# Two decoder layers with mixture-of-experts: attention's buffers share places, gate and up run in four column tiles, the gather goes through four banks

## The chip, the core and the metric

The kernel runs on one core of one Trainium2 chip. The metric is the device time of one execution in microseconds, the median of the runs shown. In the profile, PE is TensorE (PEld its weight loads), DVE is VectorE, ACT is ScalarE, POOL is GpSimd, and SP is SyncE, whose queue issues nearly all DMAs of this kernel. Times inside the trace count from the start of the span.

## The reference

Two post-norm layers work on 256 tokens of width 1024, all in float32. Layer 0 mixes tokens by sliding-window attention with sinks, layer 1 by differential attention; in both, four more heads attend to 256 memory tokens. After `x = LN(alpha*x + mix)` comes the expert block, and then `x = LN(alpha*x + moe)`. Cut to what matters here:

```python
aff = sigmoid(x @ w_router)                  # 64 experts, 8 groups
eidx = top 8 experts of the 4 best groups    # for each token
gates = aff[eidx] / sum(aff[eidx]) * 2.5
for every expert e and the tokens that chose it:
    h = silu(xb @ w_gate[e]) * (xb @ w_up[e])        # 1024 -> 256
    routed += gate * (h @ w_down[e])                 # 256 -> 1024
shared = (silu(x @ ws_gate) * (x @ ws_up)) @ ws_down
moe = routed + shared
```

Each expert has three matrices of 1 MB (1024 x 256 float32). With 64 experts and two layers that is 403 MB of the 449 MB that the kernel moves.

## The kernel before, in words

**The ring.** `store` holds the router's matrix `wr` and then 12 places of one matrix each (`ring`). Experts are worked on in pairs; a pair is one unit, and a layer has 32 of them. Even units take their six matrices from places 6 to 11, odd units from places 0 to 5 (`pair_place`, L134): two gates, two ups, two downs (`matrix_at`). So the ring holds two units. Besides it there are a few places of their own: `apart` (unit 1's second down), `up_apart` in `work` (unit 0's first up), and the four buffers `home`, `lnrow`, `xT`, `x` with `memT`, which take over one whole pair, number 16, once attention and routing have no more use for them (`keep`, L553). In steady state a place is loaded again as soon as its matrix has been used (`reload_gate`, `reload_up`, `reload_down`, L453 to L495).

**Before the experts.** During attention the same ring places hold the projection matrices (`in0` to `in3`, `memkv`, `out0`, `out1`) and the shared expert's gate and up (`shared`). Which place each has stands in `first_place` (L130), and `before_it` says after which other item it may be loaded. SP walks this list in order (L604 to L650), and each of its waits holds back everything behind it in the list. What the attention leaves occupied is loaded late: unit 1's two gates wait for the second logit group and for the end of the shared expert's up (L642, L644, semaphore `gate_apart`); `xT` and `x` are free last (L556).

**One unit on PE** (`unit`, L1410): `gate` (L1282 to L1305), `up` (L1307 to L1332), `scatter` of the unit two before (adds rows back into the token sums, L1372), `turn_back` for the next unit (L1264 to L1269), `turn_h` (L1337, transposes of the hidden rows), on every fourth unit `gather` of the next eight experts' tokens (L1236 to L1258), and `down` of the unit before (L1341 to L1366). For `gate` and `up` the stationary operand is the 64 token slots of an expert, so two experts sit side by side in two tiles of 64 columns; `down` works with tiles of 32 columns, four side by side. A float32 matmul shows up as two records in the trace, so a `gate` has 32 matmul records and 32 weight loads.

**The gather** writes eight chunks of x into PSUM banks 0, 1, 2, 0, 1, 2, 0, 1; ACT copies the even chunks out, DVE the odd ones. A chunk waits until the last one in its bank has been copied. `down` behind a gather waits for the copies of the last chunks (`xg_act` and `xg_dve`), since it writes to banks 0 and 1.

**The first reloads.** PE reports the first half of a gate (`half_gated`), and SP then loads unit 2's first gate half into the same place (`reload_gate_halves`, L521 and L523). This is the earliest load that depends on the experts' own progress.

The trace shortens some names: L848 is `product`, used for the gather and others; L1498 and L1742 are the copies of ACT and DVE.

Of the kernel before, what the change touches and what calls it, by code (L numbers as in the profile page):

```python
# [78 lines left out]
def build_trunk(nc, x_in, xT_in, memT_in, w_in_a, sinks, w_in_b, lambda_qk, subln_g, w_mem_kv, w_out, ln_g, ln_b,  # L79
# [43 lines left out]
    for l in range(DEPTH):  # L123
# [10 lines left out]
    before_it = [{"out1": "in0", "shared": "in1"}, {"out0": "memkv", "out1": "in2", "shared": "in0"}]  # L134
    pre = [[(l, name) for name in first_place[l]] for l in range(DEPTH)]
# [4 lines left out]
    with ExitStack() as ctx:  # L140
# [11 lines left out]
        store = sb("store", [P, KT * NE + 2 * REGION * MATRIX])  # L152
        wr = store[:, 0:KT * NE].rearrange("p (k n) -> p k n", k=KT)
        ring = store[:, KT * NE:]
        router_gate = store[:, 0:KT * (NE + HID)].rearrange("p (c k n) -> p c k n", k=KT, n=NE)
# [6 lines left out]
        work_at = nc.sbuf_base  # L162
        work = sb("work", [P, 8960])
# [5 lines left out]
        qT = work[:, 0:1536].rearrange("p (t n) -> p t n", n=SEQ)  # L169
        kT = work[:, 1536:3072].rearrange("p (t n) -> p t n", n=SEQ)  # L170
        v = work[:, 3072:4608].rearrange("p (t n) -> p t n", n=768)
        qmT = work[:, 4608:5120].rearrange("p (t n) -> p t n", n=SEQ)
        kmT = work[:, 5120:5632].rearrange("p (t n) -> p t n", n=MEM)
        vm = work[:, 5632:6144].rearrange("p (t n) -> p t n", n=MEM_HEADS * HD)
        mixT = work[:, 6144:8192].rearrange("p (t n) -> p t n", n=SEQ)
        heads = over("heads", [P, TT, 768], xhalf_at + 8192)
# [5 lines left out]
        yhalf = over("yhalf", [P, 2, D], work_at + 4 * 5120, F32R)  # L182
        yend = [work[:, 5120 + c:5120 + c + 256] for c in (512, 768)]
        hot8 = over("hot8", [P, TT, OCTET * TILE_SLOTS], work_at + 4 * 7168, F32R)
# [3 lines left out]
        sgs = work[:, 3584:4096].rearrange("p (t n) -> p t n", t=TT)  # L188
        hsrow = work[:, 7680:8192].rearrange("p (t n) -> p t n", t=TT)
# [6 lines left out]
        soft = [over(f"soft{i}", [P, 256], xhalf_at + 1024 * i) for i in range(3)] + [work[:, 8450:8706]]  # L196
        softT = [over(f"softT{i}", [P, 2, P], xhalf_at + at) for i, at in enumerate((4096, 5120, 14336, 15360))]
# [9 lines left out]
        negdist = over("negdist", [P, 2 * P], xhalf_at + 3072)  # L207
        apart = sb("apart", [P, FT, D])
        up_apart = work[:, 5120:7168].rearrange("p (k n) -> p k n", k=KT)
# [6 lines left out]
        lamrow = over("lamrow", [P, 4, HD], xhalf_at + 6144)  # L216
        sublnrow = over("sublnrow", [P, 2 * HD], xhalf_at + 7168)
        lamv = sb("lamv", [P, 8])
        lamp = over("lamp", [P, 2, HD], xhalf_at + 7680)
# [7 lines left out]
        passed = work[:, 5120:6144]  # L227
        route = sb("route", [P, 4, TT, NE])
# [29 lines left out]
        gather_bank = (0, 1, 2, 0, 1, 2, 0, 1)  # L258
# [14 lines left out]
        def item_loads(it):  # L273
# [6 lines left out]
            if name == "shared":  # L280
                return [(matrices(at), ws_gate[l]), (by_k(matrices(at + 1)), by_row_run(ws_up[l]))]
            if name[:3] == "out":
                return [(matrices(at, 2), w_out[l, int(name[3])])]
# [45 lines left out]
        def last_group(it):  # L329

            l, name = it
            return G[l, {"memkv": "vm", "in0": "q2" if l == 0 else "q5", "in1": "qm" if l == 0 else "k5", "in2": "vd", "in3": "qm",
                         "out0": "y2", "out1": "y3"}[name]]
# [11 lines left out]
        def used(sp, it):  # L345

            if it[1] == "shared":
                sp.wait_ge(sem(f"shared_gu_{it[0]}"), TT)
            else:
                filled(sp, last_group(it))  # L350
# [25 lines left out]
        def bank_at(g):  # L376
            return banks[bank_no[g]]
# [40 lines left out]
        def _(sp):  # L418
# [120 lines left out]
            def next_down(l):  # L539

                sp.dma_start(apart[:], w_down[l, 1, :, 1, :].rearrange("p (f n) -> p f n", f=FT)).then_inc(sem("down_apart"), 16)
                sp.sem_inc(sem(f"down_landed{RING - 1}_{l}"), 16)
                expert(l, 1, RING - 1, 2)
# [34 lines left out]

            extra = None
            for l in range(DEPTH):  # L580
                for it in pre[l]:
                    if it[1] in before_it[l]:
                        used(sp, (l, before_it[l][it[1]]))
                    elif l > 0:

                        of_pair = 0 if place_of[it] >= REGION else 1
                        sp.wait_ge(sem(f"down_done_{l - 1}"), extra * NE + (NE - RING + 2 * of_pair + 2))
                    if it == (1, "memkv"):
                        load_part(it, 0)
                        load_memory_halves()  # L590
                        load_norm(1, extra)
                        load_part(it, 1)
                    else:
                        load(it)
                    if it == (1, "in3"):
                        sp.wait_ge(sem("x_back"), TT)
# [1536 lines left out]
```

## Time and profile before

| | before |
|---|---|
| runs, us | 1186.79, 1184.7, 1186.67 |
| median, us | 1186.67 |
| span of the profiled execution, us | 1183.3 |
| median less span (what lies around the span), us | 3.4 |
| PE busy | 1149.2 us, 97% |
| DMA | 449.12 MB, mean 380 GB/s |
| granted clock of TensorE, mean | 0.996 |

The span is one profiled execution; durations below come from it. A PE that is busy 97% of the time is not a PE at its peak, since the ends of pipelined matmuls are modelled. The slices of the page show the DMA rate over the span: near 428 GB/s through both expert phases, and two stretches with far less, which are the two attentions.

### The profile page before, as it was taken

Reading aid. Unit: us, or ns where it says so; the run is one execution under the profiler, and the core shown is the slowest. Engines: PE = TensorE matmul, PEld = TensorE weight load, DVE = VectorE, ACT = ScalarE, POOL = GpSimd, SP = SyncE. Lnnn points to the kernel's source line nnn. Section 1 sums busy time; section 2 is a strip of 40 time slices with the busy share of each in tenths; the row PEclk is TensorE's granted clock in tenths of the full one; section 3 lists DMA queues with packets and bytes.
Section 4 is the critical chain, followed back from the end, with each engine's and each line's share of the span. In section 5 each row is a group of like instructions: output and inputs, shape, how many; then the busy total and the mean of one; then the engine's idle time right before and its main releaser. Section 6 shows DMA issues by size and latency. Waiting matters only on the chain.

```text
span 1183.3 us, 22174 instructions
## 1 busy us (share of the span) xinstructions
PE 1149.2 (97%) x8846; PEld 688.0 (58%) x8846; DVE 347.2 (29%) x912; ACT 300.0 (25%) x713; POOL 56.4 (5%) x100
## 2 busy tenths in 40 slices
PE   9999999999999999999999999999999899999995
PEld 6865755555555555554787647555555555555552
DVE  0445522222122212121523557221222222121224
ACT  1454222212122212121214533122221212221222
POOL 1431100000001000000011001000000010000000
PEclk9999999999999999999999999999999999999998
DMA  9945999999999999999990558999999999999995
GB/s 375 418 161 185 349 418 426 428 428 428 429 428 421 429 426 427 426 426 418 406 364 2 230 233 343 408 426 426 429 429 428 428 423 427 426 426 428 428 423 204
DMA packets 42732, 449.12 MB, mean 380 GB/s; under 512 B 4512, under 2 KB 4896, under 8 KB 14240
## 3 DMA queue, kind: packets, MB, share of 16 engines
q1 hardware_dynamic: 41648, 443.30, 89.8%
q10 hardware_dynamic: 1008, 4.73, 1.0%
q8 instruction: 57, 0.93, 0.3%
q14 instruction: 19, 0.16, 0.0%
HBM read 446.96 MB, written 1.05 MB: 379 GB/s over the span
## 4 chain that ended last, share of the span: by engine, by line
PE 85%; DMA 9%; DVE 3%; ACT 1%; issue 1%; DVEq 0%; SPq 0%; ACTq 0%
PE bank L1301 18%; PE bank L1328 17%; PE bank L1364 17%; PE bank L848 7%; PE bank L867 6%; PE bank L1372 5%; PE bank L906 4%; DMA store<-in_w_gate 4%; DMA store<-in_w_down 3%; DMA store<-in_w_in_b 2%; PE bank L1337 2%; PE bank L1196 1%; PE bank L1066 1%; PE bank L1077 1%; ACT work L1498 1%
## 5 line engine op out<-in xcount | busy, mean ns | idle before, releaser
L1301 PE MATMUL bank<-store,work 128*64 128x256 f32 x1984 | 227.8, 382 | 5.3 <-DMA store<-in_w_gate 5.3
L1328 PE MATMUL bank<-store,work 128*64 128x256 f32 x1952 | 225.3, 379 | 6.2 <-issue 6.2
L1364 PE MATMUL bank<-store,work 128*32 128x512 f32 x1888 | 218.4, 595 | 3.1 <-ACT work L1498 2.9
L1301 PEld LDWEIGHTS bank<-store,work 128*64 128x64 f32 x1984 | 137.0, 137 | 116.1 <-issue 41.1
L1328 PEld LDWEIGHTS bank<-store,work 128*64 128x64 f32 x1952 | 145.0, 137 | 75.7 <-issue 11.6
L2030 DVE SCALAR_TENSOR_TENSOR yhalf<-bank,gcol,yhalf 128x512 fp32r<-128x512 f32 x124 | 92.9, 751 | 219.1 <-ACT yhalf L1664 219.1
L2022 DVE TENSOR_TENSOR work<-work,bank 128x256 f32<-128x256 f32 x64 | 27.0, 422 | 346.9 <-PE bank L1328 346.9
L1664 ACT ACTIVATE yhalf<-bank,gcol 128x512 fp32r<-128x512 f32 x124 | 85.1, 688 | 172.1 <-PE bank L1364 172.1
L1364 PEld LDWEIGHTS bank<-store,work 128*32 128x32 f32 x1888 | 56.1, 109 | 122.4 <-issue 110.7
L1498 ACT ACTIVATE work<-bank 128x512 f32<-128x512 f32 (+4 forms) x177 | 78.0, 441 | 105.8 <-PE bank L848 47.3
L1498 ACT ACTIVATE back<-bank 128x128 fp32r<-128x128 bf16 x64 | 17.8, 278 | 282.0 <-PE bank L1269 282.0
L867 PE MATMUL bank<-xT,store 128*128 128x256 f32 x352 | 77.9, 380 | 0.7 <-DMA store<-in_w_in_b 0.7
L1372 PE MATMUL bank<-yhalf,back 64*128 64x512 f32 x504 | 75.7, 418 | 0.0
L1742 DVE COPY work<-bank 128x512 f32<-128x512 f32 (+3 forms) x77 | 51.5, 672 | 70.8 <-PE bank L848 41.2
L867 PEld LDWEIGHTS bank<-xT,store 128*128 128x128 f32 x352 | 66.2, 190 | 10.4 <-DMA store<-in_w_in_b 1.1
L1654 ACT ACTIVATE work<-bank 128x256 f32<-128x256 f32 x64 | 24.6, 385 | 184.3 <-PE bank L1301 184.3
L848 PE MATMUL bank<-hot,xhalf 128*128 128x256 f32 x512 | 69.4, 290 | 1.0 <-DVE xhalf L1895 0.9
L848 PEld LDWEIGHTS bank<-hot,xhalf 128*128 128x128 f32 x512 | 64.0, 189 | 4.6 <-issue 2.1
L1372 PEld LDWEIGHTS bank<-yhalf,back 64*128 64x128 f32 x504 | 42.4, 184 | 30.1 <-issue 23.8
L906 PE MATMUL bank<-store,work 128*128 128x512 f32 x128 | 57.8, 594 | 0.0
L906 PEld LDWEIGHTS bank<-store,work 128*128 128x128 f32 x128 | 23.2, 190 | 23.4 <-issue 23.1
L819 POOL TENSOR_TENSOR x<-xhalf 128x1024 f32<-128x1024 f32 x4 | 9.6, 2426 | 475.3 <-PE bank L1364 475.3
(185 smaller groups left out, 822.7 us busy)
## 6 DMA issues: line engine op xcount, KB each, us to landing
store<-in_w_down SPq DMA_DIRECT2D x56, 2048.0 KB, 17.7
store<-in_w_gate SPq DMA_DIRECT2D x56, 2048.0 KB, 17.7
store<-in_w_up SPq DMA_DIRECT2D x52, 2048.0 KB, 19.2
store<-in_w_up SPq DMA_DIRECT2D x18, 1024.0 KB, 10.5
store<-in_w_gate SPq DMA_DIRECT2D x12, 1024.0 KB, 8.5
store<-in_w_in_b SPq DMA_DIRECT2D x3, 3072.0 KB, 22.4
store<-in_w_out SPq DMA_DIRECT2D x4, 2048.0 KB, 14.2
store<-in_w_down SPq DMA_DIRECT2D x6, 1024.0 KB, 11.7
```

The lines of the kernel that those rows point to most:

```text
L848: last = pe.matmul(dst, a, b, start=(n == 0), stop=(n == len(pairs) - 1))
L867: mm = pe.matmul(bank_at(g)[:, c * 256:(c + 1) * 256], w[:, k, c0 + c * P:c0 + (c + 1) * P], moving[:, k, :], start=(k == 0), stop=(k == K ...
L906: last = pe.matmul(bank_at(g)[:], mixT[:, c, t * P:(t + 1) * P], item_view((l, f"out{half}"), 512)[:, c, :], start=start, stop=(done == KT))
L1301: last = pe.matmul(gate_bank[slots_of(e), 0:HID], xg[:, k, slots_of(2 * j + e)], w[e][:, k, :], start=(k == 0), stop=(k == KT - 1))
L1328: last = pe.matmul(up_bank[slots_of(e), 0:HID], xg[:, k, slots_of(2 * j + e)], w[e][:, k, :], start=(k == 0), stop=(k == KT - 1))
L1364: last = pe.matmul(yb[half][rows_of(t, e), :], hT[b][:, f, slots_of(e, t)], w[e][:, f, half * 512:half * 512 + 512], start=(f == 0), stop= ...
L1372: pe.matmul(sums[2 * t + half][:], back[b][rows_of(t), :], yhalf[rows_of(t), n, half * 512:half * 512 + 512], start=False, stop=False)
L1498: return act.activation(dst, src, ACT.Copy)
L1664: act.activation(yhalf[:, 0, half * 512:half * 512 + 512], yb[half][:], ACT.Copy, scale=gcol[:, j:j + 1])\
L1742: return dve.tensor_copy(dst, src)
L2022: dve.tensor_tensor(hidrow, sg, up_bank[:, 0:HID], ALU.mult).then_inc(s_("h_ready"), 1)
L2030: dve.scalar_tensor_tensor(out=yhalf[:, 1, part], in0=yb[half][:], scalar=gcol[:, j:j + 1], in1=yhalf[:, 0, part].bitcast(F32), op0=ALU.mu ...
```

## The change

It does four things.

1. The router's matrix moves out of `store` to the front of `work`; the ring keeps its 12 places. The soft-max buffers, `heads`, `negdist` and the like move from `xhalf` into `work`, and the row constants of layer 1 onto `route`. `xhalf` so becomes free during attention and holds the first half of the output projection (`out_first`, in place of `out0`).
2. The shared expert's gate and up go to `work[0:4096]` (where keys, values and memory keys and values lie until attention is done) in place of ring places.
3. SP's list is written out by hand for each layer. Experts' matrices whose places are now free are loaded earlier in it, among them unit 1's two gates as one load. The loads `gate_apart` and `gate_landed` behind the logits are gone.
4. On PE, `gate` and `up` issue one matmul for each 32 slots, four column tiles in place of two. The gather uses banks 0, 3, 1, 2, 0, 3, 1, 2, and the waits in and behind it are set accordingly.

The core of the diff:

```diff
-        {"in1": 0, "in0": 3, "memkv": 6, "out0": 8, "out1": 3, "shared": 0},
-        {"memkv": 6, "in1": 9, "in0": 0, "in3": 8, "in2": 3, "out0": 6, "out1": 3, "shared": 0},
+        {"in1": 0, "in0": 3, "memkv": 6, "out1": 3},
+        {"memkv": 6, "in1": 9, "in0": 0, "in3": 8, "in2": 3, "out1": 3},
...
+        out_first = over("out_first", [P, KT, 512], xhalf_at)
+        shared_w = [work[:, 0:MATRIX], work[:, MATRIX:2 * MATRIX]]
...
-        gather_bank = (0, 1, 2, 0, 1, 2, 0, 1)
+        gather_bank = (0, 3, 1, 2, 0, 3, 1, 2)
...
+            def load_shared_down(l):
+                sp.wait_ge(sem("softened"), sum(len(jobs[i]) for i in range(l + 1)))
+                sp.dma_start(shared_wd, by_row_pair(ws_down[l])).then_inc(sem("shared_wd_landed"), 16)
+
+            def load_shared(l):
+                sp.dma_start(shared_w[0], ws_gate[l]).then_inc(sem("shared_gate_landed"), 16)
+                sp.dma_start(by_k(shared_w[1]), by_row_run(ws_up[l])).then_inc(sem("shared_up_landed"), 16)
+
+            def first_layer():
...
+                load_out_first(0)
+                load_rows(0)
+                row_pair(0)
+                load_x()
+                pair(0, 0, 0, 2)
+                next_up(0)
+                expert(0, 0, 1, 1)
+                load_apart(0)
+                used(sp, (0, "in0"))
+                load((0, "out1"))
+                next_down(0)
+                used(sp, (0, "in1"))
+                pair(0, 0, 1, 0)
+                expert(0, 0, 2, 1)
+                for e in range(2):
+                    keep(0, 0, e)
+                used(sp, (0, "memkv"))
+                pair(0, 0, 0, 0)
+                keep(0, 2, 1)
+                load_shared_down(0)
+                sp.wait_ge(sem("valued"), len(products[0]))
+                load_shared(0)
+                load_up_apart(0)
+
+            def second_layer(extra):
...
+                load((1, "in2"))
+                load_out_first(1)
+                load_apart(1)
+                for e in range(2):
+                    keep(1, 0, e)
+                used(sp, (1, "memkv"))
+                pair(1, 0, 0, 0)
+                keep(1, 2, 1)
+                sp.wait_ge(sem("normed"), 2 * TT)
+                row_pair(2)
+                used(sp, (1, "in3"))
+                next_up(1)
+                used(sp, (1, "in2"))
+                load((1, "out1"))
+                next_down(1)
+                used(sp, (1, "in1"))
+                expert(1, 0, 1, 1)
+                pair(1, 0, 0, 2)
+                used(sp, (1, "in0"))
+                pair(1, 0, 1, 0)
+                expert(1, 0, 2, 1)
+                load_shared_down(1)
+                filled(sp, G[1, "heads"] + 2)
+                load_shared(1)
+                load_up_apart(1)
...
                 used(sp, (l, "out1"))
                 expert(l, 0, 3, 1)
                 expert(l, 0, 2, 2)
                 sp.wait_ge(sem("normed"), 2 * TT * l + TT)
-                load_up_apart(l)
                 keep(l, 1, 0)
-                filled(sp, G[l, "vm"])
-                keep(l, 2, 1)
-                filled(sp, G[l, "logit1"])
-                sp.dma_start(matrices(matrix_at(1, 0, 0)), w_gate[l, 1, :, 0, :]).then_inc(sem("gate_apart"), 16)
-                used(sp, (l, "shared"))
-                sp.dma_start(matrices(matrix_at(1, 1, 0)), w_gate[l, 1, :, 1, :]).then_inc(sem(f"gate_landed{UNROLL}_{l}"), 16)
+                sp.wait_ge(sem(f"shared_gu_{l}"), TT)
                 keep(l, 1, 1)
...
-                landed(pe, it)
+                pe.wait_ge(sem("shared_gate_landed"), (l + 1) * 16)
...
+                pe.wait_ge(sem("shared_up_landed"), (l + 1) * 16)
                 up_shared(0)
...
                         if k == 2 and backs is not None:
-                            pe.wait_ge(s_("hT_ready"), backs)
-                        if k == 1 and backs is not None:
                             pe.wait_ge(s_("back_ready"), backs + 1)
                             pe.wait_ge(s_("gcol_ready"), backs + 1)
+                        if k == 3 and backs is not None:
+                            pe.wait_ge(s_("hT_ready"), backs)
...
                         for e in range(2):
-                            last = pe.matmul(gate_bank[slots_of(e), 0:HID], xg[:, k, slots_of(2 * j + e)], w[e][:, k, :],
-                                             start=(k == 0), stop=(k == KT - 1))
+                            for t in range(TT):
+                                last = pe.matmul(gate_bank[slots_of(e, t), 0:HID], xg[:, k, slots_of(2 * j + e, t)], w[e][:, k, :],
+                                                 start=(k == 0), stop=(k == KT - 1))
...
-                        if half == 0:
-                            pe.wait_ge(s_("xg_act"), 4 * gathers + 1)
-                        else:
-                            pe.wait_ge(s_("xg_dve"), 4 * gathers + 1)
+                        pe.wait_ge(s_("xg_act"), 4 * gathers + half)
+                        if half == 1:
```

`up` is changed as `gate` is, with `up_bank`. ACT's copy of x into `xhalf` (`x_high`) has a new wait, for the third output group `y2`, since `out_first` lies there.

## Rows read from the trace of the kernel before

**Rows 1.** The page: DMA rate in 40 slices of the span.

```profile
GB/s 375 418 161 185 349 418 426 428 428 428 429 428 421 429 426 427 426 426 418 406 364 2 230 233 343 408 426 426 429 429 428 428 423 427 426 426 428 428 423 204
```

**Rows 2.** Busy time in stretches: layer 0's units 4 to 7, 8 to 11, 12 to 15.

```profile
core 0: us, PE busy (x) PEld busy (x) DVE busy (x) ACT busy (x) POOL busy (x), PEclk, DMA share, GB/s
182.60:235.90 53.30, 53.09 (x468) 29.81 (x464) 12.72 (x30) 12.10 (x24) 0.00 (x0) 1.00 1.01 426
235.90:289.20 53.30, 53.11 (x468) 30.18 (x464) 12.63 (x30) 12.09 (x24) 0.00 (x0) 1.00 1.01 428
289.20:347.90 58.70, 53.85 (x468) 30.86 (x464) 12.65 (x30) 12.08 (x24) 0.00 (x0) 1.00 1.01 429
```

**Rows 3.** Groups of PE instructions, 289.2 to 347.9 us: busy, mean ns, idle before.

```profile
L1364 PE MATMUL bank<-store,work 128*32 128x512 f32 x132 | 15.2, 595 | 0.2 <-ACT work L1498 0.2
L1301 PE MATMUL bank<-store,work 128*64 128x256 f32 x128 | 14.7, 382 | 1.8 <-DMA store<-in_w_gate 1.8
L1328 PE MATMUL bank<-store,work 128*64 128x256 f32 x128 | 14.6, 381 | 2.9 <-issue 2.9
```

**Rows 4.** The chain that ended last, in order of time: start, length, what.

```profile
1137.99 18.08 DMA store<-in_w_down
```

**Rows 5.** SP's issues about the start of layer 0's experts: start, length, line.

```profile
129.52 0.33 SPq L644 DMA_DIRECT2D store<-in_w_gate  x1
129.89 0.43 SPq L556 DMA_DIRECT2D xT<-in_w_up  x1
132.15 0.33 SPq L556 DMA_DIRECT2D x<-in_w_down  x1
136.28 0.68 SPq L521 DMA_DIRECT2D store<-in_w_gate  x1
```

**Rows 6.** Busy time in two stretches there, columns as in rows 2.

```profile
130.00:138.00 8.00, 7.64 (x64) 5.94 (x64) 4.72 (x11) 2.40 (x4) 3.51 (x6) 1.00 0.94 357
138.00:142.00 4.00, 3.95 (x36) 2.33 (x35) 0.60 (x4) 0.57 (x3) 0.00 (x0) 1.00 0.97 321
```

**Rows 7.** DMA issues from 103.0 to 103.6 us, 136 to 137, 734 to 735: time to landing.

```profile
store<-in_w_up SPq DMA_DIRECT2D x1, 1024.0 KB, 5.0
...
store<-in_w_gate SPq DMA_DIRECT2D x1, 1024.0 KB, 8.4
...
store<-in_w_gate SPq DMA_DIRECT2D x1, 1024.0 KB, 9.5
```

**Rows 8.** Instruction blocks among the DMAs of units 4 to 7 (182.6 to 235.9 us).

```profile
q8 instruction: 4, 0.07, 0.5%
```

**Rows 9.** DMA kinds of units 8 to 11 (235.9 to 289.2 us).

```profile
q1 hardware_dynamic: 1566, 22.81, 100.6%
q14 instruction: 1, 0.01, 0.0%
```

**Rows 10.** PE groups by shape: the last down's halves, four tiles of 32 columns.

```profile
L1397 PE MATMUL bank<-store,work 128*32 128x256 f32 x64 | 3.9, 379 | 0.0
```

**Rows 11.** PE in order of time: a gate, its up, the down behind, the next gate.

```profile
182.83 3.67 PE L1301 MATMUL bank<-store,work 128*64 128x256 f32 x32
186.33 3.62 PE L1328 MATMUL bank<-store,work 128*64 128x256 f32 x32
...
191.49 3.64 PE L1364 MATMUL bank<-store,work 128*32 128x512 f32 x32
195.06 1.30 PE L1301 MATMUL bank<-store,work 128*64 128x256 f32 x10
```

**Rows 12.** PE's end of attention in order of time, layer 0, then layer 1.

```profile
95.12 1.09 PE L1100 MATMUL bank<-softT,work 128*64 128x128 f32 x16
...
110.88 4.47 PE L1179 MATMUL bank<-store,xT 128*128 128x320 f32 x16
...
690.73 0.60 PE L1139 MATMUL bank<-ident,heads 128*128 128x128 f32 x4
...
709.23 3.12 PE L1179 MATMUL bank<-store,xT 128*128 128x320 f32 x11
```

More of the change, by code:

```diff
@@ L279, in item_loads @@
                 return parts if l == 1 else [(matrices(at, 2), w_mem_kv[l].rearrange("j p n -> p j n"))]
[L280 to L283, printed above, removed]
+            if name == "out1":
+                return [(matrices(at, 2), w_out[l, 1])]
             if it == (0, "in1"):
@@ L618, in _ @@
                 if l == 0:
-                    used(sp, (0, "memkv"))
-                    pair(0, 0, 0, 0)
-                else:
-                    used(sp, (1, "in1"))
-                    expert(1, 0, 1, 1)
-                    pair(1, 0, 0, 2)
-                sp.wait_ge(sem("softened"), sum(len(jobs[i]) for i in range(l + 1)))
-                sp.dma_start(shared_wd, by_row_pair(ws_down[l])).then_inc(sem("shared_wd_landed"), 16)
-                used(sp, (l, "out0"))
-                if l == 0:
-                    next_up(0)
-                    expert(0, 0, 1, 1)
-                else:
-                    pair(1, 0, 0, 0)
+                    first_layer()
+                else:
+                    second_layer(extra)
@@ L899, in out_part @@
                     if n not in y_begun:
-                        landed(pe, (l, f"out{half}"))
+                        if half == 0:
+                            pe.wait_ge(sem("out_first_landed"), (l + 1) * 16)
+                        else:
+                            landed(pe, (l, "out1"))
                         bank_free(pe, g)
+                    wo = item_view((l, "out1"), 512) if half else out_first
                     for c in cs:
@@ L905, in out_part @@
                         done = y_done[n] = y_done[n] + 1
-                        last = pe.matmul(bank_at(g)[:], mixT[:, c, t * P:(t + 1) * P],
-                                         item_view((l, f"out{half}"), 512)[:, c, :], start=start, stop=(done == KT))
+                        last = pe.matmul(bank_at(g)[:], mixT[:, c, t * P:(t + 1) * P], wo[:, c, :], start=start, stop=(done == KT))
                         if done == KT:
@@ L1295, in gate @@
                     for k in range(KT):
-                        if j == 0 and k == 0 and first:
-                            chunk_out(O, 3)
+                        if j == 0 and k == 0:
+                            chunk_out(O, 3 if first else 5)
                         if j == 0:
@@ L1327, in up @@
                         for e in range(2):
-                            last = pe.matmul(up_bank[slots_of(e), 0:HID], xg[:, k, slots_of(2 * j + e)], w[e][:, k, :],
-                                             start=(k == 0), stop=(k == KT - 1))
+                            for t in range(TT):
+                                last = pe.matmul(up_bank[slots_of(e, t), 0:HID], xg[:, k, slots_of(2 * j + e, t)], w[e][:, k, :],
+                                                 start=(k == 0), stop=(k == KT - 1))
                         if place == 1 and k == KT // 2 - 1:
@@ L1590, in head_out @@
                     else:
[L1591 removed]
+                        act.activation(heads[:, h, n, :], src, ACT.Copy, scale=rden[:, j - 1:j])
                         act.wait_ge(sem("headed"), m)
```

141 lines of the change are left out of this document (59 added, 82 removed).

## The prediction

> **What bounds the kernel now.** The page's slices come first [rows 1]: both expert phases run at 426 to 429 GB/s, and in each attention the rate falls far below, to 161 and to 2. So there is idle DMA time in attention, which is what earlier loads could use. The question is whether what bounds the experts is PE or the DMA. Busy time in stretches answers it [rows 2]: units 4 to 7 and 8 to 11 take 53.3 us each with PE busy almost throughout, while the DMA share is 1.01 in all three stretches, and units 12 to 15 take 58.7 us for the same 468 matmuls. PE is thus a little faster than the loads; it lives on the two units that the ring held at the start, and when that lead is used up it waits, 1.8 us ahead of gates and 2.9 us ahead of ups [rows 3]. Since the DMA engines are never idle from the first reload on, the end of such a phase is set by the bytes and by when the saturated stretch began, and PE's pace only decides where the waiting is done. The chain of waits agrees [rows 4]: the end of layer 1 goes through a down's load, 18.08 us from issue to landing. Layer 0 has the same order of loads at its end and layer 1's projections queued behind them, so I take both phases to end behind the DMA.
>
> **The change part by part.**
>
> **Earlier loads.** Per layer the bytes are the same, so a load that is moved counts only if it takes bytes out of the saturated stretch. That stretch starts with the first reload, which can't move: SP issues it at 136.28 us, when PE has done half of the first gate [rows 5]. What still lay ahead of it? Three loads of 1024 KB, issued at 129.52, 129.89 and 132.15, 3.15 MB together [rows 5]. From 130 to 138 us the engines moved 357 GB/s x 8 us = 2.86 MB [rows 6], so 0.29 MB, 0.7 us at 428 GB/s, were left at 138, and the reload began at about 138.7. A lone 1 MB load lands 5.0 us after its issue [rows 7], of which 2.45 us is the transfer; of the 2.55 us of the rest I give 1.0 to the time before the first bytes, so the reload could begin at 137.3 at best. The change takes the first of the three loads (L644, unit 1's second gate) out; the other two, 2.1 MB, need 4.9 us from 130.9 and are done by 136. The gain is 138.7 - 137.3 = **1.4 us per layer**, not the 2.45 us of the load itself, and much less than the several MB that are moved in the list: the rest of them only fill time in which the engines have nothing to do anyway. Bounds: nothing, if the second reload, which also waits for PE, leaves a hole; and at most 3.4 us in layer 0 and 4.5 in layer 1, by which the first reload lands later than the lone load (8.4 and 9.5 against 5.0 [rows 7]). I take the value by bytes, because the reload's own pieces move at only 321 GB/s [rows 6], which explains the rest of its lateness without a queue.
>
> **More instructions.** Four tiles double the matmuls and weight loads of gate and up: 32 + 32 records more for each, 128 more per unit, 512 per four units. Four units now issue 468 + 464 records [rows 2] and fetch four blocks of instructions, 0.5% of the engines' 53.3 us, 0.27 us, or 0.067 us a block [rows 8]. 512 on top of 932 make 2.2 blocks more per four units. Units 8 to 11 are the second pass of a loop and fetch none on q8 [rows 9], so six of the eight groups of four fetch: 13 blocks, 0.9 us per layer of saturated DMA. Bounds: nothing, and 1.7 us if the second and third passes (units 8 to 15) also fetch their 6.2 blocks each. The Trainium skill, "Runtime: NRT & Kernel Launch", section "Instruction fetch mechanics", says in a note that there are only two lines of 16 KB and that a taken branch out of them forces a fetch before execution goes on. By that units 8 to 11 would have fetched before too; the trace differs, and the row decides; by the page the sum would be 1.7 us later.
>
> **Four column tiles on PE.** The streaming is the same: as many columns, twice the tiles, each half as wide. The nearest row is the last down's two halves, the very form that gate and up get: 64 records in 3.9 us over two layers [rows 10], so 1.95 us for eight groups of four, less 0.16 us for the modelled end of the last, 0.22 us a group. A gate now has 16 steps in 3.50 us, 0.22 each [rows 11]. What is saved is the change of tile width: gate to up, same width, 3.50 us; down to gate 3.57 us, and that gate's first loads stand free. I take 0.1 us per unit, 3 us per layer, bounds 0 and 0.2.
>
> **Gather and its waits.** Down waits 0.2 us for ACT's copy behind a gather [rows 3], and the fourth bank removes about as much inside it: 0.4 us in seven gathers, some 3 us per layer. `down`'s first half then waits for chunk 4 alone. Neither this nor the tiles reaches the end: they make PE faster in a phase that ends behind the DMA, so they come out as longer waits for gates and ups. I cost them at nothing; what covers them is those waits, 5.4 us in units 12 to 15 already. Only behind the layer's last load is PE alone: there one change from down to up goes, 0.1 us once, in layer 1.
>
> **New waits.** SP now waits for the last values (layer 0) or the last turned heads (layer 1) before the shared gate is issued, and behind that wait stand `up_apart`, unit 1's last up and down, and the keeps. The last values end at 96.2 us, so the load lands at about 101.2; PE needs it at 110.88 for the logits, 9.7 us later [rows 12]. In layer 1: 691.3 + 5.0 = 696.3 against 709.23, 12.9 us. Moved loads ahead of it would have to hold the queue for that long, four MB; so nothing. ACT's wait for `y2` costs nothing either: ACT waits for the first norm there, which follows y0 and y1, and PE runs y2 right behind them. The moved buffers change no instruction's shape.
>
> **Sum.** Two layers: 2 x (-1.4 + 0.9) - 0.1 = -1.1 us. The profiled span of 1183.3 becomes 1182.2; with the 3.4 us that lie between span and median, 1186.67 becomes **1185.6 us**. That is under 0.2% (2.4 us), about the least that a measurement of this kernel can tell from no change.
>
> **The rivals.**
>
> A, the queue was the whole lateness: the first reload lands 3.4 and 4.5 us earlier, and all loads behind it too. For it: the engines were hardly idle from 131 us on, and PE's faster units could free places sooner. Against it: the 321 GB/s. -7.9 + 1.8 - 0.1 = -6.2: 1180.5 us.
>
> B, the longer loop no longer stays where the fetched one stayed: units 8 to 15 fetch too, 2 x 12.4 x 0.067 = 1.7 us more: 1187.3 us, and more if PE also stands at the loop's end. Against it: nothing in rows 8 and 9 tells how much room there is.
>
> C, slower: PE can't be fed with eight instructions per group over a whole gate and up, 256 in a row, where the row of the same form has 64 in a row per layer. The densest long run that waits on nothing visible is 16 matmuls with their loads in 1.09 us [rows 12], 34 ns an instruction; at that pace a group takes 0.27 instead of 0.22 us. 128 gates and ups of 16 groups are 2048 groups: 113 us, less the cover of at least 5.4 + 3 + 3 us per layer, 23 us: +90, 1277 us. It decides from 23 / 2048 = 11 ns per group on. Against it: rows 10 show no such pace. The Trainium skill, "TensorE: Matmul & The Clock Gate", section "Step-by-step: what each phase is for", tells of about 62 ns for a matmul where the sequencer's software decodes it; four would take 0.248 us a group, and the estimate by that page is 1186.67 + 2048 x 0.03 - 23, about 1225 us. The 0.22 us of rows 10 speak against that case here, though only in a short run.
>
> **How the numbers follow.** Forecast (between the bounds of its two terms, 1183 to 1187) 0.57, A 0.22, B 0.13, C 0.05, the rest 0.03 for a shared load that comes late. Faster by over 0.2%: A, and the edge of the forecast where the fetch costs nothing (-2.8 - 0.1), 0.30 together. Slower: C, the rest and the end of B where PE stands at the loop, 0.12. The range takes in A and B and their spread and leaves out C: 1180.3 to 1188.8 us.
>
> **What would show it.** Right: the first reload in each layer lands 1 to 2 us sooner after its issue; the DMA share stays 1.0 from there on; gate and up keep 3.5 us; the octets with PE ahead fall from 53.3 to about 52.5 us while PE's waits for gates and ups grow by as much; q8 counts about a third more blocks. Wrong: gates of more than 3.7 us (C), q8 blocks in the loop's later passes (B), a first reload at 5 us from issue to landing (A), or a phase whose DMA share falls below 1, which would mean that PE bounds it after all.

## The result: 4 us slower, and the profile after

The changed kernel took 1190.17 us (median of 5 runs, 1189.13 to 1190.6) against 1186.03 us for the kernel before (5 runs, 1184.38 to 1186.79): a ratio of 1.0040, 95% interval 1.0029 to 1.0051 (the two medians alone give 1.0035). The forecast was 1185.6 us, within 1180.3 to 1188.8. The profiled execution has a span of 1188.7 us and a time of 1190.48 us; the spans of the two profiles are 5.4 us apart. In the runs on record the time is some 1.8 us over the span. So the 3.4 us that the table ahead of the prediction puts around the span are 1.8 us of that and 1.6 us by which the profiled execution of the kernel before was under its median; against the median of five it is 0.9 us under, and the profile after is 0.3 us over its own. That is why the profiles are further apart than the medians (4.1 us).

Most of what the prediction named as a sign came out as it said, and yet the time went the other way. First the stretches that answer to [rows 2]: units 4 to 7, 8 to 11 and 12 to 15 of layer 0. Four units, eight experts, are called an octet below.

```profile
core 0: us, PE busy (x) PEld busy (x) DVE busy (x) ACT busy (x) POOL busy (x), PEclk, DMA share, GB/s
181.70:233.90 52.20, 52.20 (x724) 28.36 (x720) 12.68 (x30) 12.08 (x24) 0.00 (x0) 1.00 1.01 426
233.90:289.10 55.20, 52.76 (x724) 28.86 (x720) 12.62 (x30) 12.08 (x24) 0.00 (x0) 1.00 1.01 428
289.10:347.90 58.80, 53.31 (x724) 29.07 (x720) 12.75 (x30) 12.08 (x24) 0.00 (x0) 1.00 1.01 429
```

PE is faster: 52.2 us for an octet in which it does not wait, where it took 53.3. It reaches the loads sooner and then waits for them, 2.4 us already in units 8 to 11, and unit 16 starts at 347.9 us, 0.2 us sooner than before. The groups of PE instructions of 289.1 to 347.9 us (busy, mean ns, idle before) answer to [rows 3].

```profile
L1389 PE MATMUL bank<-ring,router_work 128*32 128x512 f32 x132 | 15.2, 595 | 0.0
L1355 PE MATMUL bank<-ring,router_work 128*32 128x256 f32 x256 | 14.6, 380 | 3.7 <-issue 3.7
L1327 PE MATMUL bank<-ring,router_work 128*32 128x256 f32 x256 | 14.6, 380 | 1.8 <-DMA ring<-in_w_gate 1.8
```

Twice the products in the same 14.6 us: no slower issue, so rival C is out. The wait inside the down is gone (0.2 in [rows 3], 0.0 here), the wait ahead of the ups has grown. In PE's order of time two gates whose loads are late show the pace of the loads, one gate to the next with the idle time in brackets:

```profile
315.84 3.66 PE L1327 MATMUL bank<-ring,router_work 128*32 128x256 f32 x64 [0.90 <-DMA ring<-in_w_gate]
...
330.51 3.66 PE L1327 MATMUL bank<-ring,router_work 128*32 128x256 f32 x64 [0.89 <-DMA ring<-in_w_gate]
```

14.67 us for a unit of three loads of 2 MB, 4.89 us a load: this pace of full DMA engines is used below. The first reload of each layer, issue to landing, answers to the last two of [rows 7]: 6.5 and 6.3 us instead of 8.4 and 9.5.

```profile
ring<-in_w_gate SPq DMA_DIRECT2D x1, 1024.0 KB, 6.5
...
ring<-in_w_gate SPq DMA_DIRECT2D x1, 1024.0 KB, 6.3
```

The kinds of DMA: the whole span of the kernel before and of the changed one, then the changed one's units 4 to 7 (as [rows 8]) and 8 to 11 (as [rows 9]):

```profile
q8 instruction: 57, 0.93, 0.3%
...
q8 instruction: 81, 1.33, 0.5%
...
q8 instruction: 6, 0.10, 0.8%
...
q1 hardware_dynamic: 1626, 23.64, 100.6%
q14 instruction: 1, 0.01, 0.0%
```

81 blocks of PE's instructions, where the kernel before has 57. Units 8 to 11 still fetch none, so rival B is out as well: the loop is read once, on its first pass (units 4 to 7: 6 blocks, 4 before). The other new blocks lie in code that runs once. The chain that ended last shows what has become of the time, before and after:

```profile
PE 85%; DMA 9%; DVE 3%; ACT 1%; issue 1%; DVEq 0%; SPq 0%; ACTq 0%
```

```profile
PE 78%; DMA 16%; DVE 3%; issue 2%; ACT 1%; POOL 0%; DVEq 0%; SPq 0%; POOLq 0%; ACTq 0%
```

**Where the 5.4 us lie.** Take the landings of the same loads in both profiles (issue plus time to landing) and subtract. A load that lands at 161.2 us before lands 1.1 us sooner after; the last load of 2 MB before the phase's end (548.8 before) 1.6 later. So layer 0's experts lose 2.7 us on the way. Layer 1's experts start 2.3 us late, 0.7 of it lost at the change of layers (no run here says by what); the first reloads win 0.5 back (+1.8 at 764.2), and the phase loses 3.3 again (+5.1 at 1146.3). The losses are along the two phases, with DMA engines that count as full in both kernels; the rest of the 5.4, 0.3 us, lies behind the phase. Between 232 and 349 us, and between 840 and 952 in layer 1, the landings keep their distance to those of before within 0.05 us: there the four tiles run from the loop and no block comes. So it is not the four streams as such; it is where blocks come.

For all kernels below that leave the loads' order alone, count how far the loads of a phase fall behind their pace: from a load near 161 us to one near 550 (and 766 to 1150) lie 76.5 to 78.5 loads of 2 MB; their time less 4.893 us each is the lag. Worked out from the landings and the list of blocks:

```
                                    blocks in the stretch   lag, us
                                    layer 0  layer 1        layer 0  layer 1
before                                19       18             3.4      2.9
e1   two tiles again                  19       19             3.7      3.6
e6   kept pair at unit 20             23       23             3.9      4.4
e11  before, own code                 27       27             5.5      4.7
e7   kept pair at 20, code as after   29       29             5.7      5.1
e3   columns cut                      30       29             5.2      5.4
e2   only four tiles                  30       29             5.9      5.7
after                                 30       30             6.2      6.2
```

From 18.75 blocks on average (before, e1) to 29.5 (the last four) the lag grows from 3.4 to 5.7 us: 0.21 us a block. Each line is one execution; those of e2 and e7 were 2.2 and 1.8 us over the medians of their runs. The lag also sits where the blocks are: take the loads in whose time a block starts, or in the 2 us before it, from 166 to 550 and 770 to 1150 us. In the changed kernel they hold 11.1 us of lag, and the other loads, half of all, -0.3; in the kernel before 6.2 and 0.2.

### The profile page after: what moved, and what is told of

Same layout as the page of the kernel before. It is cut to its first block, busy times and chain, and to the rows that moved or that the text cites. A ratio compares the mean times of both kernels' runs of the same rounds, so it can differ in the third digit from the quotient of the medians.

```text
span 1188.7 us, 30380 instructions
## 1 busy us (share of the span) xinstructions
PE 1140.5 (96%) x12940; PEld 666.2 (56%) x12942; DVE 347.1 (29%) x912; ACT 299.9 (25%) x713; POOL 56.3 (5%) x100
## 4 chain that ended last, share of the span: by engine, by line
PE 78%; DMA 16%; DVE 3%; issue 2%; ACT 1%; POOL 0%; DVEq 0%; SPq 0%; POOLq 0%; ACTq 0%
PE bank L1327 16%; PE bank L1355 15%; PE bank L1389 15%; DMA ring<-in_w_gate 12%; PE bank L873 7%; PE bank L892 6%; PE bank L1397 5%; PE bank L935 4%; DMA ring<-in_w_in_b 2%; DMA ring<-in_w_down 2%; PE bank L1364 1%; PE bank L1223 1%; PE bank L1094 1%; PE bank L1105 1%; PE bank L1206 1%
## 5 line engine op out<-in xcount | busy, mean ns | idle before, releaser
L1355 PE MATMUL bank<-ring,router_work 128*32 128x256 f32 x3904 | 227.6, 381 | 17.9 <-issue 17.9
L1327 PE MATMUL bank<-ring,router_work 128*32 128x256 f32 x3968 | 225.8, 379 | 8.2 <-DMA ring<-in_w_gate 8.2
L1389 PE MATMUL bank<-ring,router_work 128*32 128x512 f32 x1888 | 218.4, 595 | 0.7 <-DMA ring<-in_w_down 0.6
L1327 PEld LDWEIGHTS bank<-ring,router_work 128*32 128x32 f32 x3968 | 127.7, 110 | 119.6 <-issue 27.8
L1355 PEld LDWEIGHTS bank<-ring,router_work 128*32 128x32 f32 x3904 | 134.5, 110 | 100.3 <-issue 28.1
L2048 DVE TENSOR_TENSOR router_work<-router_work,bank 128x256 f32<-128x256 f32 x64 | 27.0, 422 | 359.5 <-PE bank L1355 359.5
L1389 PEld LDWEIGHTS bank<-ring,router_work 128*32 128x32 f32 x1888 | 56.1, 109 | 118.9 <-issue 110.7
L1523 ACT ACTIVATE router_work<-bank 128x256 f32<-128x256 f32 (+4 forms) x229 | 92.1, 420 | 116.3 <-PE bank L873 44.6
L892 PE MATMUL bank<-xT,ring 128*128 128x256 f32 x352 | 77.9, 380 | 1.7 <-DMA ring<-in_w_in_b 1.7
L892 PEld LDWEIGHTS bank<-xT,ring 128*128 128x128 f32 x352 | 66.2, 190 | 11.4 <-DMA ring<-in_w_in_b 2.1
L1768 DVE COPY router_work<-bank 128x512 f32<-128x512 f32 (+3 forms) x77 | 51.4, 672 | 67.8 <-PE bank L873 38.4
L1680 ACT ACTIVATE router_work<-bank 128x256 f32<-128x256 f32 x64 | 24.6, 384 | 181.2 <-PE bank L1327 181.2
L1364 PE MATMUL bank<-ident,router_work 128*128 128x128 f32 x128 | 29.4, 311 | 0.9 <-DVE router_work L2048 0.9
```

The costliest lines, as they stand in the source:

```text
L892: mm = pe.matmul(bank_at(g)[:, c * 256:(c + 1) * 256], w[:, k, c0 + c * P:c0 + (c + 1) * P], moving[:, k, :], start=(k == 0), stop=(k == K ...
L1327: last = pe.matmul(gate_bank[slots_of(e, t), 0:HID], xg[:, k, slots_of(2 * j + e, t)], w[e][:, k, :], start=(k == 0), stop=(k == KT - 1))
L1355: last = pe.matmul(up_bank[slots_of(e, t), 0:HID], xg[:, k, slots_of(2 * j + e, t)], w[e][:, k, :], start=(k == 0), stop=(k == KT - 1))
L1364: last = pe.transpose(hT_bank[:, f * P:(f + 1) * P], hidrow[:, f:HID:FT], ident[:])
L1389: last = pe.matmul(yb[half][rows_of(t, e), :], hT[b][:, f, slots_of(e, t)], w[e][:, f, half * 512:half * 512 + 512], start=(f == 0), stop= ...
L1523: return act.activation(dst, src, ACT.Copy)
```

## The experiments

Theory I: the blocks of added PE instructions cost the time, on the DMA engines that carry the weights. Theory S: four streams at once slow the loads. Theory R: the moved loads cost it. Theory K, that the place of one pair matters, came up later.

**Two tiles again** in the changed kernel, all else kept:

```diff
-    for t in range(TT):
-        last = pe.matmul(gate_bank[slots_of(e, t), 0:HID], xg[:, k, slots_of(2 * j + e, t)], w[e][:, k, :],
+    last = pe.matmul(gate_bank[slots_of(e), 0:HID], xg[:, k, slots_of(2 * j + e)], w[e][:, k, :],
```

and the same in `up`. Expected:

> The changed kernel with gate and up put back into two column tiles; its loads, its places in the memory and its four-bank gather stay. Theory I (the extra PE instructions come in as blocks of 16 KB through DMA engines that are full with weights, and each block makes the loads behind it later by a good part of the 0.9 to 1.1 us that it holds one engine): 57 to 59 PE blocks again instead of 81, and 1184 to 1186.5 us. Theory R (the order of the loads and the hole at 136 to 138 us cost the 4 us): 1189 to 1191 us, since all of that stays, with the instruction blocks gone and nothing won by it. Theory S (four streams at once slow the DMA writes) expects the same time as I but no tie to the blocks.

Measured: 57 blocks, 1185.79 us against 1185.56 for the kernel before on the same chip, ratio 1.0005 (0.9996 to 1.0014). So R falls: the loads, the places and the gather cost nothing. They win nothing that can be measured either. Why not is seen in the stretch in which the first reload runs, 136 to 140 us, before and then after:

```profile
136.00:140.00 4.00, 4.00 (x40) 2.46 (x36) 0.47 (x3) 0.55 (x2) 0.00 (x0) 1.00 0.99 378
```

```profile
136.00:140.00 4.00, 4.00 (x75) 2.22 (x71) 0.47 (x3) 0.55 (x2) 0.00 (x0) 1.00 0.72 197
140.00:144.00 4.00, 3.57 (x60) 2.01 (x56) 1.47 (x5) 0.66 (x2) 0.00 (x0) 1.00 0.94 311
144.00:148.00 4.00, 4.00 (x84) 2.40 (x76) 0.00 (x0) 0.38 (x1) 0.00 (x0) 1.00 0.96 356
```

The last two columns are DMA share and GB/s. The megabyte that is taken out from ahead of the reload leaves the engines idle instead (a share of 0.72, so 1.1 of the 4 us), since the reload waits for PE in any case; the next reloads wait for PE, too, and the lead of 2.1 us at the first landing is 0.6 us by the load that lands at 166 us. One of the new blocks falls into these loads as well (at 146.4 us); the two-tile run has none there, and of its lead, too, only 0.5 to 0.8 us is left.

**Only the four tiles**, in the kernel before (the diff above the other way round, for gate and up). Expected:

> The kernel before with nothing but gate and up in four column tiles; loads, places and gather as before. Theory I: 80 to 82 PE blocks, 1188.5 to 1191 us (about 4 us over before). Theory R: no slower than before, 1184 to 1187 us, although it has the blocks. Theory S: as I.

Measured: 81 blocks, 1191.62 us (1188.64 to 1193.83), ratio 1.0049 (1.0035 to 1.0062), 0.6 us over what I and S both said. The four tiles alone bring the loss; it is 2 us more than that of the whole change, but the intervals of the two ratios overlap.

**Columns cut**, in the kernel before: as many PE instructions as with four tiles, two tiles wide as before.

```diff
-    last = pe.matmul(gate_bank[slots_of(e), 0:HID], xg[...], w[e][:, k, :], start=(k == 0), stop=(k == KT - 1))
+    for c in (slice(0, P), slice(P, HID)):
+        last = pe.matmul(gate_bank[slots_of(e), c], xg[...], w[e][:, k, c],
+                         start=(k == 0 and c.start == 0), stop=(k == KT - 1 and c.start > 0))
```

> The kernel before, two column tiles, but each product of gate and up cut at column 128 into two of half the length: the same number of extra PE instructions as the change adds (64 products and 64 weight loads in a unit), and no fourth stream. Theory I: 80 to 82 PE blocks, and slower than before by 2.5 to 5.5 us, 1188.5 to 1191.5 us. Theory S (the streams, not the instructions): as before, 1184.5 to 1187.5 us. Theory R: as before.

Measured: 81 blocks, 1191.99 us, ratio 1.0055 (1.0042 to 1.0069). S falls, by a time that is 0.5 us over the range of I. The run is not quite clean: its units take 12.37 us on PE instead of 12.23, and a part of the 6.4 us may be that. So a run was wanted that adds code and nothing else.

**Own code**: the kernel before, its first PE loop written out.

```diff
-    with pe.Fori(1, RES_OCTET) as o:
-        for j in range(OCT_PAIRS):
-            unit(r, o, j)
+    for alone in range(1, RES_OCTET):
+        with pe.Fori(alone, alone + 1) as o:
+            for j in range(OCT_PAIRS):
+                unit(r, o, j)
```

> The kernel before, nothing changed in any product, load or wait, but its first PE loop of three octets written out as three octets of code of their own (62 KB each): about 8 PE blocks more in a layer. Theory I at 0.2 us for a block: 72 to 74 PE blocks instead of 57 and 1187.8 to 1189.5 us. If a block cost only its sixteenth share, 0.067 us: 1186 to 1186.8 us. If the four column tiles and not the code slowed the changed kernel: no change, 1184.5 to 1186 us.

Measured: 72 blocks, 1189.82 us, ratio 1.0038 (1.0025 to 1.0051). Not one product, load or wait is changed, and the time rises by 4.5 us for 15 blocks, 0.30 us each, a little more than the range of I had at 0.2. Units 4 to 7 and 8 to 11 of it, stretches as in [rows 2]:

```profile
182.60:235.90 53.30, 53.09 (x468) 29.83 (x464) 12.67 (x30) 12.09 (x24) 0.00 (x0) 1.00 1.01 427
235.90:289.20 53.30, 51.49 (x452) 29.80 (x452) 12.02 (x29) 11.39 (x23) 0.00 (x0) 1.00 1.01 426
```

and the DMA kinds of its units 8 to 11, where the kernel before has no line for q8 [rows 9]:

```profile
q1 hardware_dynamic: 1554, 22.64, 100.0%
q8 instruction: 4, 0.07, 0.5%
q14 instruction: 1, 0.01, 0.0%
```

PE waits in units 8 to 11 now (51.49 busy of 53.3, where it was 53.11). One more rival fits the added code: PE itself stands still until its instructions are there, and the loads have no part in it. The traces speak against it. In the phases of this run 17 gates and ups start after a wait of over 0.15 us, in the changed kernel 27, and every one of them starts within 0.25 us after a load has landed. So PE waits for weights, not for code, and this is theory I by itself.

**Fewer blocks under four tiles**: the changed kernel with the kept pair at unit 20, so that one loop takes octets 1 to 4 and the second is gone.

```diff
-RES_PAIR = 16
+RES_PAIR = 20
...
-    with pe.Fori(RES_OCTET + 1, SHARED_OCTET) as o:
-        for j in range(OCT_PAIRS):
-            unit(r, o, j)
```

> The changed kernel with the pair that is kept in the chip's memory at unit 20 instead of 16: the first PE loop then takes four octets instead of three, and one octet that ran once from code of its own (95 KB, nearly 6 blocks) is gone in each layer. Theory I: 69 to 71 PE blocks instead of 81, 1187 to 1189.3 us. Theories R and S: 1189.5 to 1191 us, no change.

Measured: 69 blocks, 1188.01 us, ratio 1.0026 (1.0016 to 1.0037): 1.7 us less over before than the changed kernel, as I said. But the kept pair (the one that stays in the buffers of attention) has moved, too, which makes theory K. Its control has the pair at unit 20 and the code of the changed kernel (the first loop ends an octet earlier, the fourth octet has a loop of one pass):

> Control for the run with the kept pair at unit 20: the changed kernel with the kept pair at unit 20 as there, but the first PE loop cut to three octets again and the fourth given code of its own, so that as much code is read as in the changed kernel. Theory I (the cost is the blocks): 80 to 82 PE blocks and 1189 to 1191 us, as the changed kernel. Theory K (the place of the kept pair won the 2 us there, whatever the code): 1187.5 to 1188.7 us.

Measured: 81 blocks, 1191.13 us, ratio 1.0049 (1.0035 to 1.0063), 0.1 us over the range of I. K falls: the place by itself wins nothing (6.03 us over before against 4.14, with intervals that overlap), and 12 blocks fewer are worth the difference of the two excesses over before, 6.03 - 2.45 = 3.6 us, 0.30 each. In both runs PE is busy without a break behind the kept pair, so the phase's end is not the loads' alone there, and this price is less clean than that of the own code.

**Attempts at a faster kernel.** If blocks cost that much, a two-tile kernel should win by taking code away. Seven runs tried; none did. First the kept pair at unit 24, in the octet with the shared expert, in three forms: the changed kernel, with two tiles, and the kernel before.

```diff
-RES_PAIR = 16
+RES_PAIR = 24
...
-        unit(r, SHARED_OCTET, j, shared=j)
+        unit(r, SHARED_OCTET, j, kept=(j == 0), kept_before=(j == 1), shared=j)
```

> The changed kernel, four column tiles, with the kept pair at unit 24, in the octet that also does the shared expert: the first PE loop takes octets 1 to 5, and two octets of code are gone in each layer. Theory I, at 0.2 us for a block (from 12 blocks and 2.2 us less in the run with the kept pair at unit 20): 57 to 59 PE blocks and 1185 to 1187 us. Theory K: 1187.5 to 1189 us.

> The changed kernel with two column tiles in gate and up and with the kept pair at unit 24 as in the run before this one: the least code of all. Theory I: 41 to 43 PE blocks and 1182 to 1184 us (1185.8 less 15 times 0.2). Theory K: 1184 to 1185.5 us.

> The kernel before with the kept pair at unit 24 and the two octets of code gone; loads, places and gather as before. Theory I: 41 to 43 PE blocks and 1182 to 1184 us, the same as the version with the changed loads, since those won nothing measurable. If the changed loads do win their 0.45 us a layer once fewer blocks are in the way, this run is 0.5 to 1 us slower than that one.

Measured: 1201.3, 1201.95 and 1204.42 us, with 58, 42 and 42 blocks; ratios 1.0137, 1.0143 and 1.0155, each within 0.0016. All three expectations were wrong: the times are 14 to 20 us over theory I's ranges. Three stretches of layer 0 in the two-tile form (the kept unit is in the second):

```profile
410.00:460.00 50.00, 44.83 (x389) 26.01 (x386) 9.20 (x24) 9.49 (x20) 0.00 (x0) 1.00 1.01 429
460.00:510.00 50.00, 50.00 (x409) 25.97 (x410) 11.96 (x25) 10.38 (x21) 4.77 (x2) 1.00 1.01 424
510.00:550.00 40.00, 40.00 (x343) 22.52 (x340) 8.72 (x20) 9.14 (x19) 0.00 (x0) 1.00 0.95 399
```

PE waits for loads up to the kept pair (44.83 of 50), which needs none; behind it PE is busy throughout and ends the phase, and the DMA runs dry (0.95). PE has lost in waits ahead of unit 24 what it would need behind it. With the pair at unit 20 the same two-tile and before kernels:

> The changed kernel with two column tiles and the kept pair at unit 20, where the last units still wait for loads (at unit 24 they no longer did, and the time rose by 16 us): one octet of code gone in each layer. Theory I: 48 to 50 PE blocks, 1183.5 to 1185 us, 1 to 2 us under the kernel before. If the four column tiles' faster PE is what lets the kept pair sit at unit 20, this run loses instead: over 1188 us.

> The kernel before with the kept pair at unit 20 and one octet of code gone; loads, places and gather as before. Theory I: 48 to 50 PE blocks and 1183.5 to 1185.5 us. The slower gather (units of 16.55 us at the end of an octet instead of 15.92 in the changed kernel) may make PE the bound behind the kept pair: then 1186 to 1190 us, over the run with the changed gather.

Measured: 49 blocks in both; 1189.29 us, ratio 1.0035 (1.0022 to 1.0049), and 1192.07 us, 1.0062 (1.0050 to 1.0074). The rivals in these expectations were right, the second in direction (it is 2 us over its range). The loads of the two-tile run are only 1.8 us behind their pace in layer 0, with 15 blocks, where those of the other two-tile run were 3.7; but PE is busy without a break behind the kept pair:

```profile
410.00:460.00 50.00, 50.00 (x442) 27.90 (x440) 12.62 (x27) 11.68 (x24) 4.78 (x2) 1.00 1.00 425
460.00:510.00 50.00, 50.00 (x412) 26.76 (x406) 8.97 (x22) 8.62 (x19) 0.00 (x0) 1.00 1.01 427
510.00:550.00 40.00, 40.00 (x344) 22.77 (x344) 9.25 (x21) 9.66 (x19) 0.00 (x0) 1.00 1.01 428
```

With four tiles and the pair at unit 20 PE is busy without a break there as well (50.00 us of 460 to 510), but in units of 12.10 us instead of 12.23. The gather may tell, too: the form with the changed gather and loads is 2.8 us faster than the one without. Last, the shared expert's part moved to the octet of the kept pair, the pair left at unit 16:

```diff
-SHARED_OCTET = OCTETS - 2
+SHARED_OCTET = RES_OCTET
...
-        unit(r, RES_OCTET, j, kept=(j == 0), kept_before=(j == 1))
+        unit(r, RES_OCTET, j, kept=(j == 0), kept_before=(j == 1), shared=j)
```

with the loop behind it over octets 5 and 6.

> The changed kernel with two column tiles and the kept pair at unit 16, where it was, but with the shared expert's last part moved from octet 6 into octet 4, the one that holds the kept pair: octets 5 and 6 then run as one PE loop, and one octet of code (62 KB) is gone in each layer, with the loads untouched. Theory I, at 0.2 to 0.3 us for a block: 49 PE blocks instead of 57 and 1183 to 1184.5 us, 1 to 2.5 us under the kernel before. If the block's cost were only that of the added ones behind a late PE: 1185 to 1186.5 us, as the two-tile run.

> The kernel before with the same move of the shared expert's last part into octet 4, its own loads, places and gather: 49 PE blocks. Theory I: 1183 to 1184.5 us. If the gather through four banks and the earlier loads win something once there is less code, this run is 0.5 to 1.5 us slower than the one before it.

Measured: 49 blocks in both; 1186.34 us, ratio 1.0011 (1.0002 to 1.0021), and 1190.48 us, 1.0045 (1.0031 to 1.0059). Theory I's range missed both. The first lies in the range of the other case that was named (1185 to 1186.5 us), the second is 4.1 us slower than the first, where 0.5 to 1.5 was expected. Stretches of the first one, from its slowest execution of eleven (1190 us):

```profile
370.00:390.00 20.00, 20.00 (x145) 9.16 (x148) 3.28 (x8) 3.56 (x8) 4.78 (x2) 1.00 1.00 424
390.00:410.00 20.00, 20.00 (x168) 12.07 (x162) 6.18 (x12) 5.59 (x11) 0.00 (x0) 1.00 0.92 380
410.00:430.00 20.00, 20.00 (x180) 11.32 (x180) 4.18 (x12) 3.30 (x8) 0.00 (x0) 1.00 1.01 414
```

The shared work makes PE 8.1 us later at unit 20 than in the two-tile run; places come free later, and the DMA has a hole at 390 to 410 us. The loads are 3.6 us behind those of the two-tile run at 428 us. From there to 550 us, with 5 blocks instead of 8, they win 1.5 us back. That fits a price on blocks, but no version that beats both kernels was found. Why the form on the loads and gather of before loses 4.1 us more was not followed up.

## Why the prediction was wrong

- **What bounds the kernel**: right. The phases end behind the DMA; faster PE came out as longer waits. The later runs make it sharper than I had it: with two tiles PE and loads end nearly together, and a few microseconds shifted to one side make PE the bound.
- **Four tiles and gather on PE**: right in kind and size. A unit takes 12.10 instead of 12.23 us (0.13; I took 0.1), the octet that is not held up 52.2 us (I said about 52.5), and none of it reaches the end.
- **More instructions**: the step that failed, by its price. 12 blocks more per layer came (57 to 81; I counted 13), only where code is read for the first time. I took 0.067 us each, the block's share of sixteen engines, 0.9 us per layer, with 1.7 as the upper bound. Measured: 2.7 and 3.3 us along the two phases, 0.21 us a block by the lag, 0.30 by the run that adds code alone. The share is an average over sixteen engines, and a load has to wait for the last of them (shown below). Even the bound only allowed for more blocks, not for a dearer one. And the range stopped short of the bounds: no gain from the loads and 1.7 us of blocks per layer make 1186.67 + 2 x 1.7 - 0.1 = 1190.0 us, over its end at 1188.8.
- **Earlier loads**: mis-sized, too. I took 1.4 us per layer, the first reload did land 2 to 3 us sooner after its issue, and 0.5 to 1.1 us were left some 20 us later, none of it in the time of the two-tile run. The lower bound named the reason, a hole where the second reload waits for PE; the DMA share of 0.72 is that hole.
- **New waits, shared loads**: nothing that shows; the two-tile run has them all and takes the time of the kernel before.
- **The sum** with measured terms: -1.1 and -0.5 for the loads, +2.7 and +3.3 along the phases and +0.7 at the change of layers is 5.1 us in place of -1.1; the profiles are 5.4 apart.
- **Rival C**: with the figures shown its first term is 2048 x 0.05 = 102 us, not 113; it was out by far either way.
- **Signs to look for**: the first reload (somewhat more than said in layer 1), gate and up, the octets and a third more blocks all came out, at a time that was wrong. The DMA share did not stay at 1.0 from the first reload on: it was 0.72 from 136 to 140 us and 0.94 to 0.96 up to 152, and that hole took much of what the earlier loads had won. None of the signs tested a block's price. The lag of the loads behind their pace would have.

**Why a block costs a multiple of its share** (0.16 to 0.30 us against 0.067). A block of 16 KB takes 0.9 to 1.1 us as one packet. Landings of the changed kernel's loads and starts of its PE blocks, us:

```
landing  425.4  430.4  435.2  440.1  445.0  449.9  454.8  459.7  464.6  470.6  475.3
spacing           4.9    4.9    4.9    4.9    4.9    4.9    4.9    4.9    6.0    4.7
blocks at 429.4, 439.2, 452.0, 458.5, 468.4
```

Four blocks pass without any delay, the fifth costs 1.1 us, of which 0.2 comes back with the next load. The traces tell why. A load's semaphore counts to 16, as many steps as there are DMA engines, and the trace has the time of each step; the load has landed with the last. The last eight steps of four of these loads, us from the load's first step:

```
430.4   1.86  2.00  2.05  2.65  3.15  3.68  3.77  4.34
435.2   1.85  1.99  2.04  3.15  3.68  3.76  4.17  4.32     2.65 has become 4.17
464.6   3.13  3.37  3.54  3.56  3.69  3.73  4.18  4.32
470.6   3.15  3.37  3.54  3.56  3.73  4.19  4.33  5.39     3.69 has become 5.39
```

A block moves one step by some 1.5 us and leaves the other fifteen alone, and the step stays late from then on. Over both phases of the changed kernel, 63 of the 68 changes from one 2 MB load to the next are, to within 0.12 us, a move of one step alone, by 1.53 us in the median. The load itself is later only if the step that moved becomes the last. That each step is one engine's is inferred; the trace does not name the engine of a packet. By that reading the engines run on independently, and a price has to be read from the last one. From the kernel before to the changed one the lag of the mean step grows by 1.0 us in each layer, close to the forecast 0.9; that of the last step grows by 2.7 and 3.3. It is then also a matter of which steps the blocks meet that the price per block differs between runs (0.16 us from the changed kernel against its two-tile form, 0.30 in the cleanest).

The Trainium skill, "Runtime: NRT & Kernel Launch", section "Instruction fetch mechanics", has the sequencer fetch ahead in blocks of 16 KiB over a DMA queue of its own and calls the cost of crossing a block's boundary mostly hidden. From PE it was hidden: in units 4 to 7 of the changed kernel, with 6 blocks, it was busy for all of the 52.20 us. From the loads it was not. The section also names full unrolling as what kernels prefer; here the run that wrote a loop out lost 4.5 us.

## What to carry to other kernels

Where the DMA engines are full, instructions that are run from code of their own are paid for in loads: count added blocks at 0.2 to 0.3 us here (0.16 to 0.30 in these runs), not at a sixteenth of their time, and put added instructions into loops that are read once. Before an engine is made faster, ask whether the form that makes it faster has more instructions; speed on an engine that waits buys nothing, and its code is not free. A load taken out from ahead of a transfer that waits for something else leaves a hole and no gain. And a price that is an average share needs an upper bound in which the whole block stands in the way: loads wait for the engine that is last, not for the mean.

## What was not expected of the hardware

24 blocks of 16 KB came for 48 units with 128 instructions more each: 64 bytes an instruction. The changed PE loop, with 1444 products and weight loads in a pass, is then over 92,000 bytes, and it fetched nothing on its later passes. A fetch of PE's code slows transfers of 2 MB by more than its bytes: 24 blocks are 0.4 MB, 0.9 us at 428 GB/s, and the phases lost 6.0 us. A block that takes 0.9 to 1.1 us as a packet puts one of a load's sixteen steps back by 1.5 us, and it stays back in the loads that follow.
